# The order of the weight loads in a mixture-of-experts loop: the next expert's first weights ahead of this one's second weights, for all 32 experts

## The reference

```python
hn = rms_norm(x, norm_ffn_g[layer])
x = x + moe_ffn(hn, router_w, router_b, w_gu, b_gu, w_down, b_down)
...
def expert_block(args):
    xb, e = args
    gu = xb @ w_gu[e] + b_gu[e]                 # w_gu[e]: 1024 x 2048
    x_glu = jnp.minimum(gu[:, :D_EXPERT], SWIGLU_LIMIT)
    x_lin = jnp.clip(gu[:, D_EXPERT:], -SWIGLU_LIMIT, SWIGLU_LIMIT)
    act = x_glu * jax.nn.sigmoid(SWIGLU_ALPHA * x_glu) * (x_lin + 1.0)
    return act @ w_down[e] + b_down[e]          # w_down[e]: 1024 x 1024
```

## Time and profile before

| | |
|---|---|
| runs, us | 1238.77, 1239.41, 1240.3 (median 1239.41) |
| profiled execution, us | 1242.82 |
| its span, first to last instruction, us | 1241.0 |
| TensorE busy | 1128.7 us, 91% |
| VectorE, ScalarE, GpSimd busy | 342.2, 220.3, 223.0 us |
| mean granted TensorE clock | 0.982 of full |
| moved from memory | 448.00 MB |

### The profile page before, as it was taken

One profiled execution on the slowest core, in us unless ns is written; L12 is line 12 of the kernel. 1 busy time (PEld: TensorE's weight loads), 2 busy tenths in 40 slices (PEclk: granted clock), 3 DMA queues, 4 the chain that ended last, 5 costly groups with the idle time before them and its releaser, 6 DMA issues.

```text
span 1241.0 us, 17621 instructions
## 1 busy us (share of the span) xinstructions
PE 1128.7 (91%) x7410; PEld 584.3 (47%) x7410; DVE 342.2 (28%) x595; ACT 220.3 (18%) x361; POOL 223.0 (18%) x99
## 2 busy tenths in 40 slices
PE   7969879999999998898989999999999998988985
PEld 7859779999433333333333333343333333333332
DVE  5982686332411122111111111131111111111112
ACT  5336735634200000000000000000000000000001
POOL 5938966685000000000000000000000000000000
PEclk8989989999999999999999999999999999999998
DMA  8434426669899999999999989999999999999993
GB/s 247 177 135 144 145 86 253 236 209 418 368 421 427 428 428 429 429 428 428 429 428 428 429 361 430 429 427 429 428 429 428 429 429 427 430 428 428 428 428 167
DMA packets 54238, 450.01 MB, mean 363 GB/s; under 512 B 7136, under 2 KB 9248, under 8 KB 29472
## 3 DMA queue, kind: packets, MB, share of 16 engines
q1 hardware_dynamic: 54064, 449.06, 87.6%
q0 software_dynamic: 144, 0.52, 0.1%
HBM read 448.00 MB, written 1.05 MB: 362 GB/s over the span
## 4 chain that ended last, share of the span: by engine, by line
DMA 43%; PE 39%; issue 7%; POOL 5%; DVE 3%; ACT 1%; SPq 1%; POOLq 0%; DVEq 0%
DMA gu<-in_w_gu 23%; DMA dn<-in_w_down 20%; PE ps L684 12%; PE ps L649 11%; POOL w_lo L373 5%; PE ps L625 3%; PE ps L426 2%; PE ps L422 2%; PE ps L423 2%; PE ps L592 2%; PE ps L672 1%; ACT w_hi L739 1%; SPq L261 1%; PE ps L446 1%; PE ps L441 1%
## 5 line engine op out<-in xcount | busy, mean ns | idle before, releaser
L649 PE MATMUL ps<-gu,xg 128*64 128x512 f32 x2048 | 453.5, 594 | 39.0 <-DMA gu<-in_w_gu 39.0
L649 PEld LDWEIGHTS ps<-gu,xg 128*64 128x64 f32 x2048 | 143.2, 137 | 331.2 <-issue 251.6
L684 PE MATMUL ps<-dn,actT 128*64 128x512 f32 x1024 | 234.9, 611 | 26.9 <-DMA dn<-in_w_down 26.7
L373 POOL TENSOR_TENSOR w_lo<-land,w_hi 128x1024 fp32r<-128x1024 f32 x80 | 217.8, 2748 | 76.0 <-ACT w_hi L739 75.9
L1195 DVE TENSOR_SCALAR g<-ps 128x512 f32<-128x512 f32 x32 | 22.1, 692 | 730.4 <-PE ps L649 730.4
L684 PEld LDWEIGHTS ps<-dn,actT 128*64 128x64 f32 x1024 | 71.7, 140 | 186.5 <-issue 143.2
L422 PE MATMUL ps<-x_hi,w_hi 128*128 128x256 f32 x384 | 98.0, 291 | 10.8 <-ACT w_hi L739 5.8
L887 ACT ACTIVATE wT<-ps 128x256 f32<-128x256 f32 x32 | 12.3, 384 | 488.8 <-PE ps L657 488.8
L423 PE MATMUL ps<-x_lo,w_hi 128*128 128x256 f32 x384 | 96.8, 288 | 0.0
L739 ACT ACTIVATE w_hi<-land 128x1024 fp32r<-128x1024 f32 x80 | 80.1, 1052 | 53.1 <-PE ps L426 39.4
L893 ACT ACTIVATE y_sb<-ps 128x512 f32<-128x512 f32 x32 | 19.1, 597 | 365.4 <-PE ps L684 365.4
(11 more groups left out here) (246 smaller groups left out, 889.9 us busy)
## 6 DMA issues: line engine op xcount, KB each, us to landing
gu<-in_w_gu SPq DMA_DIRECT2D x128, 2048.0 KB, 28.0
dn<-in_w_down SPq DMA_DIRECT2D x64, 2048.0 KB, 23.3
land<-in_w_in SPq DMA_DIRECT2D x13, 2048.0 KB, 8.1
land<-in_w_proj_rnn SPq DMA_DIRECT2D x2, 2048.0 KB, 8.8
land<-in_w_proj_attn SPq DMA_DIRECT2D x2, 2048.0 KB, 8.8
land<-in_w_out SPq DMA_DIRECT2D x2, 2048.0 KB, 7.7
land<-in_w_in SPq DMA_DIRECT2D x2, 1024.0 KB, 10.3
x_sb<-in_x SPq DMA_DIRECT2D x2, 512.0 KB, 3.9
```

Source lines behind the costliest of these rows:

```text
L373: pool.tensor_tensor(w_lo[:, q % PIECES], land[q // PIECES][:, :, (q % PIECES) * P:(q % PIECES + 1) * P], w_hi[:, q % PIECES].bitcast(f32) ...
L649: last = mm(ps[64 * h:64 * h + 64, 4 + c, :], xg[:, k * SLOTS:(k + 1) * SLOTS], gu[par][m][:, r, c * D + h * HALF:c * D + (h + 1) * HALF], ...
L684: last = mm(ps[64 * h:64 * h + 64, 6, :], actT[:, j, half * SLOTS:(half + 1) * SLOTS], dn[half][:, j, h * HALF:(h + 1) * HALF], start=half ...
```

## The change

The constant `TURN` and the second loop go. The loop with the first order now runs over all pairs, i = 1 to 15, and the load of the last expert's second weights follows behind it:

```diff
-TURN = 8
...
-            with sp.Fori(1, TURN, 1) as i:
+            with sp.Fori(1, N_E // 2, 1) as i:
                 load_gu(i * (2 * D), 0, lambda m: sp.wait_ge(gu_used, 4 * (2 * i) + (m + 1 - 8)))
                 load_dn(i * (2 * D) - D, lambda h: sp.wait_ge(dn_used, 4 * i + (h + 1 - 4)))
                 load_gu(i * (2 * D) + D, 1, lambda m: sp.wait_ge(gu_used, 4 * (2 * i) + (m + 1 - 4)))
                 load_dn(i * (2 * D), lambda h: sp.wait_ge(dn_used, 4 * i + (h + 1 - 2)))
-            load_dn((2 * TURN - 1) * D, lambda h: sp.wait_ge(dn_used, 4 * TURN + (h + 1 - 4)))
-
-            with sp.Fori(TURN, N_E // 2, 1) as i:
-                load_pair(2 * i, i * (2 * D))
+            load_dn((N_E - 1) * D, lambda h: sp.wait_ge(dn_used, 2 * N_E + (h + 1 - 4)))
```

## The result

| | before | after |
|---|---|---|
| median of the runs, us | 1239.86 (4 runs, 1238.77 to 1240.65) | 1251.02 (4 runs, 1250.33 to 1252.6) |
| profiled execution, us | 1242.82 | 1250.33 |
| its span, us | 1241.0 | 1248.6 |
| mean granted TensorE clock | 0.982 | 0.969 |

The changed kernel is slower. The medians differ by 11.2 us; the ratio is 1.0095, 95% interval 1.0079 to 1.0111, which is 9.8 to 13.8 us. The forecast was 1249.6 in 1247.6 to 1252.7.

What follows compares the result with a forecast made beforehand. The prediction took the weight stream to set the pace, 29.364 us per expert. The last L684 would end at 1237.1 instead of 1226.8, +10.2 us on 1239.4, giving 1249.6 us, range 1247.6 to 1252.7.

Steps and rivals of the forecast that it cites:

- Term 3: Last experts: from L684 of expert 30 to the end of L684 of expert 31, 34.5 us, ending at 1237.1 us.
- Term 1: Turn at expert 16: the break in the weight stream, where gu(16) stood behind dn(15), goes; -4.8 us of stream.
- The second sum: By the stream: its end moves from 1219.5 to 1214.7, TensorE's work beyond it grows from 7.3 to 22.4; +10.3 us.
- The first sum: End of the last L684, 1237.1 us in the changed kernel against 1226.8 before: +10.2 us.
- The stream deciding: Rival: the final work stays hidden, only the turn's 4.8 us count, so faster, 1234.6 us; chance 0.04.
- no change: Rival: the unbroken stream runs 0.64 us per expert faster and makes up the loss; 1239.4 us, chance 0.03.
- dn(31) late: Rival: at the end dn(31) lands late, so the last L684 ends 3.1 us later; 1252.7 us, chance 0.04.
- The clock paid each time: Rival: sixteen more experts each pay 1.7 us for a lower clock behind waits, 27 us; 1276.6 us, chance 0.01.
- No slice under 420 between 12 and 39: Sign for the stream's break gone: no page slice from 12 to 39 has a rate under 420 GB/s.

Runs made afterwards that it cites:

- turn15: Kernel before with the turn to the second load order moved from before expert 16 to before expert 30; 1243.62 us, ratio 1.0029 to the kernel before.
- after_short: Changed kernel with 24 of 64 matmuls of expert 31's first product left out, no transfer changed; 1245.89 us, ratio 1.0046 to the kernel before.
- before_short: Kernel before with 24 matmuls of expert 31's first product left out; 1241.87 us, ratio 1.0010 to the kernel before.
- smooth8b: Kernel before, loads at the turn interleaved: gu(16) tiles 0,1, dn(15), gu(16) 2,3, gu(17) 0, dn(16), gu(17) 1-3, dn(17); 1236.62 us, ratio 0.9973.
- after_warm: Changed kernel with eight small bf16 matmuls ahead of the wait for dn in experts 2 to 29; 1251.63 us, ratio 1.0092 to the kernel before.

## Why the prediction was right

*The mechanism.* Each step was seen: the same pace to the last expert (17 periods from 701.39 to 1200.61 are 29.366 us each, 29.364 forecast), the turn's break gone, the two dn pairs in a row moved to the end, and expert 30's second product and all of expert 31's work bare there. turn15 and after_short measure the bare work from two sides, before_short shows that the second order covers it.

*Term 3*, 34.5 us from L684 of expert 30 to the end, measured 1234.88 - 1200.61 = 34.3. dn(31) was in time, as said. The end lies at 1234.9 and not 1237.1 mainly because this execution began its experts 1.9 us earlier; that offset is no part of what the change costs.

*Term 1* was mis-sized: "-4.8 us of stream". By landings it is -3.4 with a dip at expert 14 and -2.8 to -3.05 without; filling it measured -3.3, doubling it +3.5. The step that failed is to turn the mean rate over one hole of one execution into time: that hole came out between 2.9 and 4.8 us from trace to trace, and in this one 0.6 MB had been moved ahead. That single engines among the 16 had been ahead and then idled is my reading of it and isn't shown.

*The second sum*, "-4.8 + 15.1 = +10.3", was no check of the first. Its 15.1 comes from the stream's end at 1214.7, which is 1219.5 - 4.8, so the 4.8 cancels and any size of the break would have given the same. Both halves were off. The stream ended near 1216.5, which is 1218.5 on the clock of the first trace (1.96 us later at L684 of expert 14): 1.0 us earlier than before and not 4.8. TensorE worked 18.4 us beyond it and not 22.4. The break had moved to the end with the two dn pairs, where dn(31) waits for dn(30) to be used; the forecast itself had dn(31) there only "by 1217". The bare end is best measured against smooth8b, which has neither cost: from L684 of expert 14 to the last L684's end the changed kernel takes 504.1 us and smooth8b 490.0, so it costs 14.1.

*The first sum*, +10.2, was made from starts and ends of TensorE and didn't rest on 4.8, but on one execution of before: 494.1 us from L684 of expert 14. The second trace has 1223.17 - 730.34 = 492.8. The 1.3 us between them are mostly the longer break of the first (0.6) and the hitch of 0.6 us near 1206 that the forecast named. With the second trace the difference is 504.1 - 492.8 = 11.3; the medians say 11.2. The hitch's cause isn't known, and that 11.3 comes so near is one trace of each and in part luck.

*The rivals.* The stream deciding (1234.6) and no change (1239.4) are out by the interval. dn(31) late is refuted by TensorE's rows. The clock paid each time (1276.6) is out by the time, and after_warm shows that the dips cost nothing.

*What was to be seen.* "No slice under 420 between 12 and 39" holds to 38; slice 39 has 362, since the queue ran dry there, the break that had stood at the turn.

## What to carry to other kernels

In a loop that is bound by its loads, the order of the loads is free in the middle and decides at the end: ask what the compute engine still has to do once the last piece that it waits for has landed, and let the long piece of work wait for the early load. Turn to the order with the short end soon enough that the compute engine can catch up (here two pairs before the end were enough, one was not), and look for where the turn makes the queue wait for a buffer with nothing else outstanding; a load or two pulled ahead of that wait fills it. Don't price such a hole from one trace: here its mean rate gave 2.9 to 4.8 us and the landings behind it 2.8 to 4.3; an edit that fills it and one that doubles it gave 3.3 and 3.5.

## What the runs showed of the hardware

Leaving out 24 of an expert's matmuls made a kernel 1.2 us slower (1.0002 to 1.0019): TensorE's waits grew to 2.69, 2.95 and 1.97 us, the granted clock behind the last two was 0.65 and 0.72, and the last 16 matmuls took 4.99 us where they take 3.65. Behind waits of 1.1 to 1.3 us groups of 16 matmuls took 3.65 us in all thirteen traces from 430 us on. Ahead of L684 none of the 57 waits of 1.84 to 1.91 us was followed by a dip, and 67 of the 100 waits of 1.92 to 2.16 us were. And one hole in the queue measured 4.8 us by the mean rate and 3.4 by the landings behind it, in the same trace.
